# Scan mixer's parameters made in the feed-forward stage before it; decay rows spread by one-pass matmuls; squares added on VectorE

## The reference, cut to what matters

```python
h = rms_norm(x, norm1_g) * (1 + sc1) + sh1;  proj = h @ w_in          # q k v, indexer, z, xbc, dt, gates
a_cs = cumsum(dt * -exp(a_log)); decay = exp(a_cs[l] - a_cs[s])        # one row a_cs per head, 32 heads
y = (C B^T * decay) @ (x * dt) + d_skip * x                            # state-space mixer (SSD)
y = rms_norm over groups of 512 channels of (y * silu(z))              # 4 groups: the "gates"
x = x + g1 * mixed;  h = rms_norm(x, norm2_g) ...;  x = x + g2 * (conv/silu(h @ w_up)) @ w_down
```

```python
lam = complex(min(lam_re, -1e-4), lam_im); step = exp(log_dt); lam_bar = exp(lam * step)
b_bar = (lam_bar - 1) / lam * b
states = scan(s[t] = lam_bar * s[t-1] + b_bar * u[t]);  y = Re(states @ c) + d * u; gelu; gated
```

## Time and profile before

| what | value |
|---|---|
| median of 3 runs | 2456.28 us |
| the profiled execution | 2457.06 us, its span 2455.0 us |
| TensorE busy | 2300.1 us (94%) |
| VectorE / ScalarE / GpSimd busy | 1772.0 (72%) / 1362.2 (55%) / 266.8 us (11%) |
| chain that ended last | PE 76%, DVE 16%, ACT 3%, POOL 2% |
| stages in us of the span | 0: 49.5 to 503, 1: to 704, 2: to 1156, 3: to 1358, 4: to 1712, 5: to 1907, 6: to 2262, 7: to 2455 |

### The profile page before, as it was taken

The page is one execution under the profiler, slowest core; times in us unless marked ns, Lnnn a source line. Parts: engine busy times, 40 slices in busy tenths (PEclk is TensorE's granted clock), DMA queues, the critical chain, the costliest instruction groups (busy, mean ns, idle before and its releaser), DMA issues.

```text
span 2455.0 us, 42466 instructions
## 1 busy us (share of the span) xinstructions
PE 2300.1 (94%) x17392; PEld 2144.8 (87%) x17392; DVE 1772.0 (72%) x3151; ACT 1362.2 (55%) x2140; POOL 266.8 (11%) x308
## 2 busy tenths in 40 slices
PE   2999999999999999999999898898999888898999
PEld 2988899999988898999999786798999775798999
DVE  5797668578659877675674889885654988886653
ACT  3577886466446888754664436444543436444542
POOL 0000000022000000000110243300000333300000
PEclk9999999999989999999999899999999899899999
DMA  7544456556645454564655413243555313243553
GB/s 278 172 165 163 155 187 213 185 188 229 227 166 168 152 187 149 186 220 144 188 174 182 135 59 107 95 149 118 189 189 172 121 61 107 94 155 122 188 186 124
DMA packets 110849, 395.73 MB, mean 161 GB/s; under 512 B 12320, under 2 KB 13888, under 8 KB 110400
## 3 DMA queue, kind: packets, MB, share of 16 engines
q1 hardware_dynamic: 96768, 343.52, 42.3%
q0 software_dynamic: 12160, 44.08, 5.5%
q10 hardware_dynamic: 1728, 5.43, 0.6%
HBM read 391.93 MB, written 1.05 MB: 160 GB/s over the span
## 4 chain that ended last, share of the span: by engine, by line
PE 76%; DVE 16%; ACT 3%; POOL 2%; issue 2%; DMA 1%; SPq 0%; DVEq 0%; ACTq 0%
PE bank L524 76%; DVE WL L1360 3%; ACT scr L933 1%; DMA ring<-in_w 1%; DVE arena L1424 1%; ACT L924 1%; POOL arena L2033 1%; PE bank L595 1%; POOL arena L2037 0%; POOL arena L2035 0%; DVE scr L1407 0%; DVE arena L1528 0%; DVE scr L1527 0%; ACT WH L933 0%; DVE arena L1958 0%
## 5 line engine op out<-in xcount | busy, mean ns | idle before, releaser
L933 ACT ACTIVATE WH<-ring 128x1024 fp32r<-128x1024 f32 (+1 forms) x638 | 670.1, 1051 | 894.5 <-PE bank L524 869.5
L524 PE MATMUL bank<-HTH,WH 128*128 128x256 f32 x3392 | 1000.7, 295 | 42.6 <-DVE HTL L1400 14.9
L524 PE MATMUL bank<-HTL,WH 128*128 128x256 f32 x3392 | 977.0, 288 | 0.0
L524 PE MATMUL bank<-HTH,WL 128*128 128x256 f32 x3392 | 976.3, 288 | 0.0
L1360 DVE TENSOR_TENSOR WL<-ring,WH 128x1024 fp32r<-128x1024 f32 (+2 forms) x616 | 745.1, 1217 | 202.2 <-ACT WH L933 200.6
L524 PEld LDWEIGHTS bank<-HTH,WH 128*128 128x128 f32 x3392 | 667.6, 197 | 75.6 <-issue 54.7
L524 PEld LDWEIGHTS bank<-HTL,WH 128*128 128x128 f32 x3392 | 669.5, 197 | 2.0 <-issue 1.4
L524 PEld LDWEIGHTS bank<-HTH,WL 128*128 128x128 f32 x3392 | 668.3, 197 | 0.0
L924 ACT ACT_TABLE_LOAD x114 | 146.3, 1283 | 47.3 <-PE bank L524 22.5
L524 PE MATMUL bank<-scr,cst 128*128 128x256 f32 (+2 forms) x304 | 96.4, 446 | 53.6 <-ACT scr L933 53.4
L524 PE MATMUL bank<-ff2h,WH 128*128 128x256 f32 x512 | 145.4, 284 | 0.0
(11 more groups left out here) (274 smaller groups left out, 3865.2 us busy)
## 6 DMA issues: line engine op xcount, KB each, us to landing
ring<-in_w SPq DMA_DIRECT2D x620, 512.0 KB, 3.7
arena<-in_wada POOLq DMA_DIRECT2D x80, 512.0 KB, 4.8
ring<-in_w SPq DMA_DIRECT2D x16, 384.0 KB, 3.7
arena<-in_wada SPq DMA_DIRECT2D x8, 512.0 KB, 19.4
arena<-in_wada ACTq DMA_DIRECT2D x8, 512.0 KB, 21.8
ring<-in_w SPq DMA_DIRECT2D x8, 288.0 KB, 2.8
arena<-in_s POOLq DMA_DIRECT2D x4, 512.0 KB, 4.1
cst<-in_cst SPq DMA_DIRECT2D x1, 1025.0 KB, 6.2
```

Source lines behind the costliest of these rows:

```text
L524: ins = e.matmul(out, a, b, start=(start and i == 0), stop=(stop and i == len(pairs) - 1))
L933: return e.activation(out, a, func, **kw)
```

## The change

Four parts, with the new line numbers of VectorE's loop and others following from them.

1. `s5` is cut in two. `s5set`, the eight pieces that make the parameters, moves to the end of the stage before (units 48 to 62 of stage 3, 38 to 52 of stage 5), with scratch in `scr[:, 0..2]`; the loads of `s5` and `wgate` move with it on GpSimd (unit 36), and GpSimd makes the tables of tiles 0 and 1 before the stage begins. The main pieces run from unit 6 in steps of 1.6 units (before: from 11 in steps of 1.5). The arena is laid out anew and `SG` moves to `trig`.
2. The decay rows are split in an fp32r pair, 32 rows high and 32 rows low (`csr`, 128x256 with zeros below); ACT makes the high rows, DVE the low rows; one one-hot pair of `picks` in fp32r spreads both in one matmul.
3. ACT squares two chunks in one operation; DVE adds the squares of chunks 0 to 5 in one tile, and one matmul sums them; stage 7 has none of it.
4. In the gates DVE adds the two tiles of squares, and 2 matmuls stand where 4 stood.

```diff
-    "s5": [1, 2, 3, 4, 5, 6, 7, 8] + turn_ticks(11, 32, 3, 2) + [59, 60, 61, 62, 63],
+    "s5": turn_ticks(6, 32, 8, 5) + [57, 58, 59, 60, 61],
 }
+S5_TICKS = {stage_b: [48, 50, 52, 54, 56, 58, 60, 62], stage_d: [38, 40, 42, 44, 46, 48, 50, 52]}
...
# TensorE: cumulative decays in two copies of 32 rows, picks, gates, sums
-                mm(b[0:32, 256:512], [(adt[:, 0:32], tri)], stop=False)
-                mm(b[0:32, 384:512], [(adt[:, 32:64], low)], start=False).then_inc(L.P.inc("cs", l), 1)
+                mm(b[0:64, 256:512], [(adt2[:, 0:64], tri)], stop=False)
+                mm(b[0:64, 384:512], [(adt2[:, 64:128], low)], start=False).then_inc(L.P.inc("cs", l), 1)
...
-                            pick = con("id", rows_=32)[:, 2 * c + hh:2 * c + hh + 1].to_broadcast([32, 128])
-                            ins = mm(L.b[0][:, hh * T:hh * T + T], [(pick, csT)])
+                            pick = picks[:, 2 * c + hh:2 * c + hh + 1].to_broadcast([128, 128])
+                            ins = mm(L.b[0][:, hh * T:hh * T + T], [(pick, csr[:, :])])
...
-                p.wait_ge(L.A("gsq", l, g))
-                for j in range(4):
-                    ins = mm(L.b[1][:, 0:T], [(con("ones"), L.s[j // 2][:, T * (j % 2):T * (j % 2) + T])],
-                             start=(j == 0), stop=(j == 3))
-                ins.then_inc(L.P.inc("gss", l, g), 1)
+                p.wait_ge(L.V("gsq", l, g))
+                mm(L.b[1][:, 0:T], [(con("ones"), L.s[0][:, T * j:T * j + T]) for j in range(2)]).then_inc(
+                    L.P.inc("gss", l, g), 1)
...
-                if g and g.kind == "res" and g.gi < 3:
-                    for c in (2 * g.gi, 2 * g.gi + 1):
-                        p.wait_ge(norm_scalar("sq", g.stage + 1, c))
-                        sums(c, square_tile(c), g.stage + 1)
+                if g and g.kind == "res" and g.gi == 2 and g.stage < 7:
+                    p.wait_ge(norm_vector("sq", g.stage + 1, 2))
+                    sums(5, square_sum, g.stage + 1, start=True)
...
# ScalarE: two chunks squared at once, high rows of the decays
+                elif s == 1 and k == "res" and gi < 3 and st < 7:
+                    p.wait_ge(residual_ready(st + 1, 2 * gi + 1))
+                    if gi == 2:
+                        p.wait_ge(norm_vector("sq", st + 1, 0))
+                    act(scr[:, 5 + gi % 2, :], flat(XT[:, 2 * gi:2 * gi + 2, :]), ACT.Square).then_inc(
+                        norm_scalar.inc("sq", st + 1, 2 * gi + 1), 1)
...
+                p.wait_ge(L.P("cs", l))
+                act(csr[0:64, :], L.b[0][0:64, 256:512], ACT.Copy).then_inc(L.A.inc("cshi", l), 1)
...
# VectorE: squares added, low rows, gates
+                elif s == 1 and k == "res" and st < 7:
+                    p.wait_ge(norm_scalar("sq", st + 1, 2 * gi + 1))
+                    t = scr[:, 5 + gi % 2, :]
+                    if gi == 0:
+                        ins = e.tensor_tensor(square_sum, t[:, 0:T], t[:, T:512], ALU.add)
+                    else:
+                        p.wait_ge(norm_vector("sq", st + 1, gi - 1))
+                        serial(e.tensor_tensor(square_sum, square_sum, t[:, 0:T], ALU.add), norm_vector)
+                        ins = e.tensor_tensor(square_sum, square_sum, t[:, T:512], ALU.add)
+                    ins.then_inc(norm_vector.inc("sq", st + 1, gi), 1)
...
-                p.wait_ge(L.P("cs", l))
+                p.wait_ge(L.P("cs", l), L.A("cshi", l))
                 e.tensor_copy(ncs, L.b[0][:, 0:64])
-                e.tensor_copy(csT, L.b[0][0:32, 256:512]).then_inc(L.V.inc("cs", l), 1)
+                e.tensor_tensor(csr[32:64, :], L.b[0][32:64, 256:512], csr[32:64, :].bitcast(F32),
+                                ALU.subtract).then_inc(L.V.inc("cs", l), 1)
...
+                p.wait_ge(L.A("gsq", l, g))
+                e.tensor_tensor(L.s[0], L.s[0], L.s[1], ALU.add).then_inc(L.V.inc("gsq", l, g), 1)
...
# GpSimd: loads and first tables in the stage before
-                    if u == plan.base[4 + 2 * l]:
-                        p.wait_ge(h_ready(4 + 2 * l, 7))
+                    if u == plan.base[3 + 2 * l] + 36:
+                        p.wait_ge(h_ready(3 + 2 * l, 7))
                         e.dma_start(flat(SC5), io["s5"][l, 0]).then_inc(s5_in.inc(by=16), 16)
                         e.dma_start(flat(SB5), io["s5"][l, 1]).then_inc(s5_in.inc(l, by=16), 16)
                         e.dma_start(wgate, io["wgate"][l]).then_inc(wgate_in.inc(l, by=16), 16)
+                    if u == plan.base[4 + 2 * l] - 1:
+                        turns(l, (0, 1))
+                    if u == plan.base[4 + 2 * l]:
+                        p.wait_ge(h_ready(4 + 2 * l, 7))
                         e.memset(AT.rearrange("p a b c -> p (a b c)"), 0.0).then_inc(LA.G.inc(), 1)
                         e.memset(SF.rearrange("p a b c -> p (a b c)"), 0.0).then_inc(LA.G.inc("zero", l), 1)
-                        turns(l)
+                        turns(l, range(2, 8))
```

More of the change, by code:

```diff
@@ L359, in program @@
         nsc = sb("nsc", [128, 16])
+        small_at = int(nc.sbuf_base)
         small = sb("small", [128, 1200])
+        csr = nc.alloc_sbuf_tensor_at("csr", [128, T], F32R, offset=small_at + 4 * 400)
+        picks = sb("picks", [128, 32], F32R)
         ring = sb("ring", [128, NSLOT, SLOT])
@@ L488, in program @@
                             agenda.setdefault(plan.base[st] + s, []).append((name, l))
+        for l in range(2):
+            st = 3 + 2 * l
+            for s in S5_TICKS[STAGES[st][0]]:
+                agenda.setdefault(plan.base[st] + s, []).append(("s5set", l))
         ada_at = {}
@@ L525, in mm, with sums @@
                 return ins
-            def sums(c, tile, st, n=8):
-                ins = mm(bank[4][:, 0:T], [(con("ones"), tile)], start=(c == 0), stop=(c == n - 1))
+            def sums(c, tile, st, start):
+                ins = mm(bank[4][:, 0:T], [(con("ones"), tile)], start=start, stop=(c == 7))
                 ins.then_inc(sums_done.inc("sum", st, c), 1)
@@ L535, in boundary @@
                         p.wait_ge(in_cst("in"))
-                    sums(c, square_tile(c), st)
+                    sums(c, square_tile(c), st, start=(c == 0))
             def attn(l, L, par):
@@ L758, in s5 @@
                 L = LC
-                for i in range(8):
-                    yield
                 def inputs(q, h):
@@ L954, in boundary @@
                     if c >= 4:
-                        p.wait_ge(sums_done("sum", st, c - 4))
+                        p.wait_ge(sums_done("sum", st, c - 4) if st == 0 else norm_vector("sq", st, 1))
                     act(square_tile(c), XT[:, c, :], ACT.Square).then_inc(norm_scalar.inc("sq", st, c), 1)
@@ L1005, in evac @@
                     act(HTH[:, c, :], GA[:, c, :], ACT.Copy).then_inc(ev_scalar.inc("mixhi", l, gi), 1)
-                elif s == 1 and k == "res" and gi < 3:
-                    for c in (2 * gi, 2 * gi + 1):
-                        p.wait_ge(residual_ready(st + 1, c))
-                        if c >= 4:
-                            p.wait_ge(sums_done("sum", st + 1, c - 4))
-                        act(square_tile(c), XT[:, c, :], ACT.Square).then_inc(norm_scalar.inc("sq", st + 1, c), 1)
+                elif s == 1 and k == "res" and gi < 3 and st < 7:
[4 more added lines that the diff above has]
+                        norm_scalar.inc("sq", st + 1, 2 * gi + 1), 1)
                 elif k == "up":
@@ L1283, in s5 @@
                     yield
+            def s5(l):
+                L = LC
                 def tanh(cc):
@@ L1325, in scalar_program @@
             act(trig[:, 0, :], y, ACT.Sin).then_inc(start_scalar.inc("trig"), 1)
+            p.wait_ge(in_cst("in"))
+            for r in (slice(0, 32), slice(32, 64)):
+                act(picks[r, :], con("id")[r, r], ACT.Copy).then_inc(start_scalar.inc(*(("pick",) if r.start else ())), 1)
             live = {}
@@ L1848, in s5 @@
                 cre, cim = (SC5[:, i, :].rearrange("p (a b) -> p a b", b=32) for i in range(2))
-                w0, w1, w2 = (t.rearrange("p (a b) -> p a b", b=32) for t in L.s)
+                w0, w1, w2 = (scr[:, i, :].rearrange("p (a b) -> p a b", b=32) for i in range(3))
                 crb, cib = (t.unsqueeze(2).to_broadcast([128, 16, 32]) for t in (cr, ci))
@@ L1861, in s5 @@
                 tab = [TF[:, i, :].rearrange("p (a b) -> p a b", b=16) for i in range(4)]
-                m0, m1 = (L.s[0][:, 256 * i:256 * i + 256].rearrange("p (a b) -> p a b", b=16) for i in range(2))
+                m0, m1 = (scr[:, 0, 256 * i:256 * i + 256].rearrange("p (a b) -> p a b", b=16) for i in range(2))
                 for which in range(2):
@@ L1884, in s5 @@
                             yield
+            def s5(l):
+                L = LC
+                V, r = L.V, s5c(1)
                 sets = [(L.s[0], L.s[1], L.b[0]), (L.s[2], SX, L.b[1])]
@@ L2021, in turns @@
                 p.wait_ge(LC.V("tf", l))
```

(2 more changed lines are left out.)

36 lines of the change are left out of this document (24 added, 12 removed), and 4 rows, old and new, of the table IK.

## The result

| kernel | median, us | ratio to before, 95% interval |
|---|---|---|
| before | 2457.26 (2456.2 to 2459.9, 4 runs) | |
| changed | 2402.19 (2399.25 to 2403.22, 4 runs) | 0.9772 [0.9755, 0.9789] |

A forecast was written before the change was run, and what follows sets the result against it. TensorE bounds stages 0 to 3, 5 and 7, VectorE stages 4 and 6. Savings 16.0 + 20.7 + 42 less 6.3 give 72.4 us, so 2384; own range 2374 to 2396, whole range 2364 to 2414.

The forecast's parts named there:

- the shorter stages 0 and 2: Sign that the forecast is right: stages 0 and 2 about 12 us shorter.
- Sums and gates: TensorE, fewer fp32 matmuls for sums of squares and in eight gates: 16.0 us saved by sums, 6.9 by gates.
- Picks: TensorE, stages 0 and 2: 0.62 us saved a pair, 13 of 16 pairs counting in each stage, 16.1 us.
- nine tenths kept: Gates and picks together cut from 23.0 to 20.7 us, because ScalarE and VectorE stand close behind TensorE in places.
- the low halves stay ahead, and I cost it at nothing: Parameters moved to feed-forward stage ends: VectorE may be 6.4 us late, so no cost; up to 24 a stage without cover.
- cost (1): End of stage 3: eighth parameter piece runs after res2's residual, so TensorE's sum waits 1.0 us, once.
- Cost (2): Boundary to stage 4: GpSimd's tables of two tiles slow eight VectorE operations, 3 us, between 0 and 6.5.
- Cost (3): Boundary to stage 6: the parameters' sine forces a ScalarE table load not there before, 1.3 us.
- net 18 us less on VectorE by unit 22 ... I take 16: Stages 4 and 6, first stretch: VectorE loses net 18 us of work, TensorE gains 16 a stage.
- 5 for the second stretch: Stages 4 and 6, 1500 to 1580 in stage 4: scan pieces thinner and ahead, two fewer, 5 us gained a stage.
- the scan eats it: Rival, stages 4 and 6: scan pieces keep VectorE full, TensorE gains only 10 a stage, 2406 us; chance 0.18.
- the 1 us for the high rows of the decays: Cost of VectorE waiting for the decays' high rows, together with the longer adt: 1 us.

The follow-up runs named there:

- the experiment above: Changed kernel with stage 3's eight parameter pieces at units 34 to 59, three to four apart, with scratch slots of their own: 2397.23 us, ratio 0.9756.
- the scan from 11 and from 14 on: Changed kernel with stage 3's parameter pieces at units 34 to 59 and the scan's first piece at unit 11 or 14: 2380.5 and 2400.22 us.

## Why the prediction was right, and where it was not

The mechanisms were right in the main, and that 2402 is as near as 18 us is in part luck: stages 0 and 2 gave 6 us more than their terms, stage 3 lost 5.4 and stages 4 and 6 lack 14. Of the signs that the prediction named, the shorter stages 0 and 2 and the cheaper pick pairs came; stages 4 and 6 some 20 us shorter, stage 3 no longer than before, L1782's mean near 480 ns (L1816 now, 625) and a boundary to stage 4 longer by 2 to 4 us (0.3) did not. TensorE idled 7.9 us in the first 95 of stage 4, where under 5 was named up to unit 22.

**Sums and gates.** Right, and a little too large. At the end of stage 0 the sum of chunks 4 and 5 still lies in front of a wait for ScalarE, 1.19 us from start to start (1.18 in the earlier trace rows):
```profile
483.39 0.64 PE L534 MATMUL bank<-scr,cst 128*128 128x256 f32 x2
484.58 1.13 PE L534 MATMUL bank<-scr,cst 128*128 128x256 f32 x4 [0.55 <-ACT scr L941]
```
A gate, measured to the second matmul behind it, went from 1.84 (second matmul at 374.41) to 1.09:
```profile
375.46 1.13 PE L534 MATMUL bank<-scr,cst 128*128 128x256 f32 x4 [0.18 <-DVE scr L1712]
376.24 0.47 PE L534 MATMUL bank<-HTH,WH 128*128 128x256 f32 x1
376.55 0.28 PE L534 MATMUL bank<-HTL,WH 128*128 128x256 f32 x1
```
0.75 saved, 8 x 0.75 = 6.0 for 6.9. Alone the two gave 19.1 of 22.2. By the profile (16.5) what is missing is spread over the stages, most of it in stage 2 (2.8 of 4.8) and stage 4 (0.4 of 1.7); no place stands out beyond what one profile can tell.

**Picks: the mechanism right, the size too small.** The term was 26 x 0.62. The 0.62 took 0.86 for the fp32 pair, from the sums; the pair's own next rows, of the kernel before, say otherwise (start, duration):
```profile
162.56 0.39 PE L524 MATMUL bank<-HTH,WH 128*128 128x256 f32 x1
162.78 0.28 PE L524 MATMUL bank<-HTL,WH 128*128 128x256 f32 x1
```
and changed:
```profile
161.80 0.50 PE L534 MATMUL bank<-csr,picks 128*128 128x256 f32 x2
162.14 0.28 PE L534 MATMUL bank<-HTH,WH 128*128 128x256 f32 x1
162.25 0.28 PE L534 MATMUL bank<-HTL,WH 128*128 128x256 f32 x1
```
From the pick's start to the second matmul behind it: 162.78 - 161.51 = 1.27 before, 162.25 - 161.80 = 0.45 now. 0.82 a pair, and 24 of the 26 later pairs read so (1.27 or 1.28 before, 0.44 to 0.46 now; the fifth pair of each stage takes some 0.76). 24 x 0.82 + 2 x 0.52 = 20.7, where stages 0 and 2 of the kernel with picks alone gave 22.0. The row was at hand; I priced by a neighbour instead of by the operation itself. And "nine tenths kept" took off a tenth for ScalarE that no run shows.

**Stage 3: "the low halves stay ahead, and I cost it at nothing".** In letter it held: TensorE waited 0.5 us for L1377. But the room was read from one slice, 3.19 busy us in 10. The kernel before has more there:
```profile
1285.00:1295.00 10.00, 10.00 (x86) 10.00 (x85) 8.28 (x15) 5.44 (x10) 0.00 (x0) 1.00 0.52 159
...
1275.00:1355.00 80.00, 78.97 (x646) 78.20 (x644) 41.53 (x56) 35.63 (x49) 2.41 (x1) 1.00 0.56 178
```
41.53 of 80 is 5.2 in 10, and 8.28 in the fullest slice. 24 us more over 15 units of 2.88 are 5.6 in 10 on top. So VectorE was full in the changed kernel:
```profile
1280.00:1290.00 10.00, 10.00 (x87) 10.00 (x86) 9.72 (x16) 4.31 (x5) 0.00 (x0) 1.00 0.32 100
1290.00:1300.00 10.00, 10.00 (x87) 10.00 (x86) 9.52 (x53) 4.20 (x5) 0.00 (x0) 1.00 0.59 200
1300.00:1310.00 10.00, 8.70 (x70) 8.10 (x68) 9.66 (x44) 4.32 (x5) 0.00 (x0) 1.00 0.54 169
1310.00:1320.00 10.00, 5.70 (x30) 5.52 (x31) 6.81 (x14) 0.31 (x2) 8.21 (x9) 0.66 0.53 170
```
The residual of res2 came late, the eighth piece stood behind it, a low half behind that, and then the adds, which GpSimd's tables (from 1311.55 on) stretched from the 0.42 of res1's to 0.84 and 0.72. VectorE, then TensorE:
```profile
1307.10 0.87 DVE L1391 SCALAR_TENSOR_TENSOR XT<-bank,mod,XT 128x256 f32<-128x256 f32 x2
...
1311.51 1.23 DVE L1377 TENSOR_TENSOR WL<-ring,WH 128x1024 fp32r<-128x1024 f32 x1
1312.65 0.84 DVE L1493 TENSOR_TENSOR scr<-scr 128x256 f32<-128x256 f32 x1
1313.53 0.72 DVE L1494 TENSOR_TENSOR scr<-scr 128x256 f32<-128x256 f32 x1
```
```profile
1314.30 1.22 PE L534 MATMUL bank<-scr,cst 128*128 128x256 f32 x2 [5.10 <-DVE scr L1494]
```
So cost (1), forecast at 1.0, was 5.1 us of waiting, and behind it TensorE had a mean granted clock of 0.66 in the slice from 1310 to 1320, so it ran part of it at 1.2 GHz after standing still: by stage, +4.3 against the -2.2 of the sums. With the pieces further apart (the experiment above) both the wait and the slow stretch are gone. The step that failed is that I looked for who waits for the low halves, and not for who waits for what else VectorE has in its queue there.

**Cost (2), GpSimd at the boundary.** Forecast at 3, found at 3.4 with the parameters alone. In the changed kernel the wait in stage 3 had pushed the boundary back, so the tables, from 1311.55 to 1331.8, were all but done when the norm began at 1331.3: L1424 has a mean of 513 ns against 479, 0.3 us. One cost hid the other, which is luck. The Trainium skill (GPSIMD Engine Reference, Specifications) has GpSimd's SBUF interfaces shared with VectorE, with contention for instructions that have two SBUF inputs. The traces agree: 744 against 479 ns on VectorE in the kernel with the parameters alone, and 417 against 417 on ScalarE.

**Cost (3), the table load.** As forecast. ScalarE at the boundary to stage 6, before and changed:
```profile
1903.77 0.47 ACT L933 ACTIVATE scr<-bank,cst 128x256 f32<-128x256 f32 x1 [0.89 <-PE bank L524]
```
```profile
1864.30 1.28 ACT L932 ACT_TABLE_LOAD   x1 [0.88 <-PE bank L534]
1865.59 0.47 ACT L941 ACTIVATE scr<-bank,cst 128x256 f32<-128x256 f32 x1
```
1.29 us from the load's start to the next operation. The Trainium skill (ScalarE: Activation LUTs, What ACT_TABLE_LOAD costs) adds a drain of some 1.38 us to each load. It does not show here either: ScalarE's idle time ahead is 0.88 us with the load and 0.89 without it.

**Stages 4 and 6: the term that failed.** It read "net 18 us less on VectorE by unit 22 ... I take 16", and 5 for the second stretch. The rows of the first 95 us give the parts. The pieces drawn forward were priced right: VectorE is 80.41 - 71.02 = 9.4 us busier with them, for the forecast 10. Without them it is 19.2 us less busy than before, and TensorE gains 14.4 us of progress, near the 16. With them 9.8 us less remain, not 18, and TensorE gains 9.2. So what failed is the size of the net, since a TensorE that gets further in the same time hands VectorE more low halves: 120 records are 5 units, whose low halves take 5 x 1.23 = 6.2, and 24 and the 2.0 of the norms less 6.2 are 19.8, where 19.2 was measured. The 24 us that leave are not 24 us of room. The rest of the stage, where the lead was to give 5, brings 10.9 - 9.2 = 1.7. The early pieces are also why L1816 (L1782 before) went from 882 not to 480 but to 625: they drew GpSimd's tables of tile 2 (1376.38 to 1388.05) over the last two of the five norms (from 1377.35 on, 842 ns at most). With the scan from 11 on it is 481:
```profile
L1816 DVE SCALAR_TENSOR_TENSOR arena<-arena,cols,scr 128x256 f32<-128x256 f32 x5 | 2.2, 481 | 3.8 <-ACT scr L941 3.8
```
The rival "the scan eats it" (22 us less, 2406) named this mechanism. Its time is nearer to the 2402 measured than the forecast is, but its size was too large: with the scan from 11 on, stages 4 and 6 give back 3.3 and 4.1 us by the profile and the kernel 11 by the median, about half of the 14 that these stages lack, where the rival put 22. That 2406 comes within 4 us is luck in part: stage 3's loss and the picks' gain, which it doesn't hold, cancel. What stays open: the three parts alone change stage 4 by -0.8 us in all, and together by -10.9 (in stage 6 by -12.9 and -16.4). 3.1 of that is the boundary (3.4 less 0.3); no run settles the other 7, and four profiles, each with a few us of its own, stand in the comparison. Nor was the 1 us for the high rows of the decays tried by itself.

## What to carry to other kernels

Price an operation by its own rows, up to the second instruction behind it. Room for moved work is a mean over the whole place and its fullest slice, and everything else queued on that engine there has its own reader: ask who waits for each. When work leaves a saturated stretch, don't fill the gap in the same edit: here the change was worth 11 us more with the scan's old list.

## What the runs showed of the hardware

- An fp32 pick of two matmuls (four records) costs 1.05 us up to the next start, and the fp32r matmul behind it is followed 0.22 us later and not 0.12; two one-pass matmuls cost 0.34 in place of 1.05. Each repetition of them costs 0.12 (six records: 162.69 to 163.50; two: 161.80 to 162.14).
- GpSimd's tables (TENSOR_TENSOR, 128x256) stretch VectorE's operation with two SBUF tensors and a column from 479 to 744 ns in the mean of eight, and the one with two tensors from 418 to 584. They run beside the first six of the eight only; ScalarE's operation stays at 417.
- The same instructions in another order of 37 places moved stage 6 between 335.8 and 346.0 us (the scan from 11 and from 14 on; one profile each).
